# First two weight tiles of the input projection worked in two token parts, with the first loads and the splits put in another order

## What is computed

```python
def rms_norm(x, g):
    xf = x.astype(jnp.float32)
    y = xf * lax.rsqrt(jnp.mean(xf * xf, axis=-1, keepdims=True) + NORM_EPS)
    return (y * g.astype(jnp.float32)).astype(x.dtype)
...
h = rms_norm(xp, norm_mix_pre[l])
z = h @ w_in
```

## Time and profile before

| | |
|---|---|
| median of 3 runs | 893.11 us (892.37 to 893.71) |
| the profiled execution's own time | 894.82 us |
| its span in the trace | 893.0 us |
| PE busy | 865.8 us, 97% |
| DVE busy | 474.3 us, 53% |
| ACT busy | 303.6 us, 34% |
| granted TensorE clock, mean | 0.988 of full |

### The profile page before, as it was taken

How to read it: one execution, slowest core, us unless ns; L and a number is a source line. 1 busy time by engine, 2 the same in 40 slices (tenths; PEclk the granted TensorE clock), 3 DMA queues, 4 the chain that set the end, 5 groups by cost and what they waited for, 6 DMA issues and landing times.

```text
span 893.0 us, 16412 instructions
## 1 busy us (share of the span) xinstructions
PE 865.8 (97%) x6866; PEld 850.1 (95%) x6866; DVE 474.3 (53%) x729; ACT 303.6 (34%) x448; POOL 69.0 (8%) x53
## 2 busy tenths in 40 slices
PE   6999999999999999999996899999999999999997
PEld 6999999999989999999995899999999999999997
DVE  6325779776735546656426654774433443334434
ACT  5211645354531112335323342123311332123432
POOL 1000101100020000000224400000000000000122
PEclk9999999999999999999996999999999999999999
DMA  9322212221313131123231022232222222322212
GB/s 311 105 95 94 86 59 72 88 90 59 96 48 101 54 101 49 54 95 95 95 94 49 18 79 95 95 94 95 82 64 89 94 94 94 94 91 66 80 48 101
DMA packets 77405, 77.28 MB, mean 87 GB/s; under 512 B 2912, under 2 KB 75120, under 8 KB 77360
## 3 DMA queue, kind: packets, MB, share of 16 engines
q1 hardware_dynamic: 68416, 70.53, 24.5%
q10 hardware_dynamic: 8304, 3.95, 1.6%
q0 software_dynamic: 640, 2.17, 0.7%
HBM read 71.64 MB, written 4.99 MB: 86 GB/s over the span
## 4 chain that ended last, share of the span: by engine, by line
PE 92%; DVE 5%; issue 1%; DMA 1%; ACT 1%; SPq 0%; DVEq 0%; ACTq 0%
PE acc L715 76%; PE wk L715 3%; PE wk L739 3%; PE wk L844 3%; DVE act_lo L1372 1%; DMA x_nat<-in_x_prompt 1%; PE wk L805 1%; PE wk L806 1%; PE wk L914 1%; DVE scaled L1353 1%; PE wk L922 1%; DVE w_lo L1065 1%; PE wk L912 0%; PE acc L1043 0%; PE acc L1045 0%
## 5 line engine op out<-in xcount | busy, mean ns | idle before, releaser
L452 ACT ACTIVATE w_hi<-w_raw 128x1024 fp32r<-128x1024 f32 x123 | 130.4, 1060 | 473.8 <-PE acc L715 455.5
L715 PE MATMUL acc<-act_hi,w_hi 128*128 128x272 f32 x1200 | 254.6, 294 | 10.8 <-DVE act_lo L1372 8.6
L715 PE MATMUL acc<-act_hi,w_lo 128*128 128x272 f32 x1200 | 249.8, 290 | 0.0
L715 PE MATMUL acc<-act_lo,w_hi 128*128 128x272 f32 x1200 | 249.1, 289 | 0.0
L715 PEld LDWEIGHTS acc<-act_hi,w_hi 128*128 128x128 f32 x1200 | 190.2, 190 | 16.0 <-DVE act_lo L1372 10.0
L715 PEld LDWEIGHTS acc<-act_lo,w_hi 128*128 128x128 f32 x1200 | 190.3, 190 | 0.0
L715 PEld LDWEIGHTS acc<-act_hi,w_lo 128*128 128x128 f32 x1200 | 188.9, 190 | 0.0
L1065 DVE TENSOR_TENSOR w_lo<-w_raw,w_hi 128x1024 fp32r<-128x1024 f32 x123 | 151.7, 1233 | 35.5 <-ACT w_hi L452 35.0
L715 PE MATMUL acc<-mid_hi,w_hi 128*128 128x272 f32 x480 | 99.0, 287 | 0.0
L715 PE MATMUL acc<-mid_hi,w_lo 128*128 128x272 f32 x480 | 98.7, 288 | 0.0
L715 PE MATMUL acc<-mid_lo,w_hi 128*128 128x272 f32 x480 | 98.6, 287 | 0.0
(11 more groups left out here) (219 smaller groups left out, 985.4 us busy)
## 6 DMA issues: line engine op xcount, KB each, us to landing
w_raw<-in_w_in SPq DMA_DIRECT2D x44, 512.0 KB, 4.4
w_raw<-in_w_ff_up SPq DMA_DIRECT2D x32, 512.0 KB, 4.7
w_raw<-in_w_ff_down SPq DMA_DIRECT2D x32, 512.0 KB, 4.0
w_raw<-in_w_o SPq DMA_DIRECT2D x8, 512.0 KB, 4.5
x_nat<-in_x_prompt SPq DMA_DIRECT2D x4, 512.0 KB, 5.7
w_raw<-in_w_attn_out SPq DMA_DIRECT2D x4, 512.0 KB, 3.6
w_raw<-in_w_ret_out SPq DMA_DIRECT2D x4, 512.0 KB, 4.5
out_y_prompt<-x_nat SPq DMA_DIRECT2D x3, 512.0 KB, 3.1
```

The source lines that it names most:

```text
L452: act.activation(w_hi[:, v % 2], w_raw[:, v // 2, :, P * (v % 2):P * (v % 2) + P], ACT.Copy).then_inc(hi_ready, 1)
L715: ins = pe.matmul(dst[:, n, 0:HALF], w[:, k, :], h[:, HALF * n:HALF * n + HALF], start=begin, stop=end)
```

## The change

The first two weight tiles are worked in two token parts (`PARTS`: tokens 0 to 255, that is x tiles 0 and 1, and tokens 256 to 543, x tiles 2 to 4). PE makes, for weight tile 0 and part 0, first the eight high x high products, then transposes x tile 3, then the products with the low weights, then those with the low x; it transposes x tile 4, does the same for weight tile 1 and part 0, and then part 1 of both tiles. `spread(0)` stands two slabs before the end of the last of these. The loads stand in the order x 0, x 1, first weight tile, x 2, 3, 4, second weight tile, next two weight tiles, key cache. ACT squares x tiles 2 and 3, DVE squares 0, 1 and 4; the squares of tiles 3 and 4, the root and the reciprocal stand behind the splits. `act_hi` and `act_lo` are made in 8 slabs of 256 and 8 of 288 tokens. DVE empties the two tiles in two pieces each.

```diff
@@ sync (SP)
+            load_x(0)
+            load_x(1)
             sp.dma_start(w_raw[:, 0, :, 0:P], w_in_v[:, :, 0:P]).then_inc(w_first, 16)
+            for t in range(2, 5):
+                load_x(t)
             sp.dma_start(w_raw[:, 0, :, P:STAGE], w_in_v[:, :, P:STAGE]).then_inc(w_in_sem[0], 16)
+            load(1, w_in_v[:, 0:4], w_in_v[:, 4:8], STAGE)
             sp.dma_start(k_cache[:], a["cache_attn_k"].rearrange("(t p) c -> p t c", p=P)).then_inc(cache_k_in, 16)
-            load(1, w_in_v[:, 0:4], w_in_v[:, 4:8], STAGE)
@@ scalar (ACT)
+            def x_high(part, copied_act, copied_dve):
+                s, n = PARTS[part]
+                act.wait_ge(x_copied_act, copied_act)
+                act.wait_ge(x_copied_dve, copied_dve)
+                for k in range(KT):
+                    act.activation(act_hi[:, k, s:s + n], xT[:, k, s:s + n], ACT.Copy, scale=gains[:, 0, k:k + 1]).then_inc(x_hi, 1)
+            copy_x(0)
+            act.wait_ge(w_first, 16)
+            split_hi(0, 0)
             act.wait_ge(var_clear, 1)
-            square_sum(1)
-            copy_x(0)
+            square_sum(2)
+            act.wait_ge(gains_in, 16)
+            x_high(0, 1, 1)
+            split_hi(1, 1, 32)
+            copy_x(2)
+            copy_x(4)
+            x_high(1, 3, 2)
             act.wait_ge(x_sum_act, 1)
             square_sum(3)
-            copy_x(2)
-            copy_x(4)
             root(0)
...
@@ tensor (PE)
+            def part_product(j, part, k, w, h, start=False, stop=False):
+                s, n = PARTS[part]
+                return pe.matmul(acc[j][:, part, 0:n], w[:, j, k, :], h[k][:, s:s + n], start=start, stop=stop)
+            def first_part(j):
+                pe.wait_ge(hi_ready, j + 1)
+                for k in range(KT):
+                    pe.wait_ge(x_hi, k + 1)
+                    part_product(j, 0, k, w_hi, H_HI, start=k == 0)
+                if j == 0:
+                    transpose_x(3)
+                pe.wait_ge(lo_ready, j + 1)
+                for k in range(KT):
+                    part_product(j, 0, k, w_lo, H_HI)
+                for k in range(KT):
+                    pe.wait_ge(x_lo, k + 1)
+                    part_product(j, 0, k, w_hi, H_LO, stop=k == KT - 1)
+            def second_part(j):
+                for k in range(KT):
+                    if j and k == KT - 2:
+                        pe.wait_ge(x_copied_act, 3)
+                        spread(0)
+                    pe.wait_ge(x_hi, KT + k + 1)
+                    part_product(j, 1, k, w_hi, H_HI, start=k == 0)
+                    part_product(j, 1, k, w_lo, H_HI)
+                    pe.wait_ge(x_lo, KT + k + 1)
+                    ins = part_product(j, 1, k, w_hi, H_LO, stop=k == KT - 1)
+                ins.then_inc(mm_done, 1)
+            first_part(0)
+            transpose_x(4)
+            first_part(1)
+            second_part(0)
+            second_part(1)
@@ vector (DVE)
             square_sum(0)
-            square_sum(2)
+            square_sum(1)
             copy_x(1)
+            split_lo(0, 0)
+            x_low(0)
+            copy_x(3)
+            split_lo(1, 1)
+            x_low(1)
             square_sum(4)
...
```

More of the change, by code:

```diff
@@ L302, in x_psum @@
                 return wk[:, 1024 * (t - 2):1024 * (t - 1)].rearrange("p (k c) -> p k c", k=KT)
-            return acc[0][:, 0, 0:KT * n].rearrange("p (k c) -> p k c", k=KT)
+            return wk[:, 0:KT * n].rearrange("p (k c) -> p k c", k=KT)
         PART_TILES = (range(0, 2), range(2, 5))
@@ L330, in _, with load_x @@
         def _(sp):
-            for t, (s, n) in enumerate(TILES):
+            def load_x(t):
+                s, n = TILES[t]
                 src = a["x_prompt"][0, s:s + n, :] if t < 4 else a["x_sample"][0]
@@ L482, in root @@
                 act.activation(tok_rstd[:, cols], tok_var[:, cols], ACT.Sqrt).then_inc(std_ready, 1)
-            act.wait_ge(var_clear, 1)
-            square_sum(1)
-            copy_x(0)
+            def x_high(part, copied_act, copied_dve):
[7 more added lines that the diff above has]
+            split_hi(0, 0)
+            act.wait_ge(var_clear, 1)
+            square_sum(2)
[5 more added lines that the diff above has]
+            x_high(1, 3, 2)
             act.wait_ge(x_sum_act, 1)
             square_sum(3)
-            copy_x(2)
-            copy_x(4)
             root(0)
[L493 to L501, removed]
             split_ahead(0, 0)
@@ L742, in _, with transpose_x @@
             pe.wait_ge(ident_in, 16)
-            for t, (s, n) in enumerate(TILES):
+            def transpose_x(t):
+                s, n = TILES[t]
                 pe.wait_ge(x_in[t], 16)
                 if t == 4:
-                    pe.wait_ge(x_copied_act, 1)
+                    pe.wait_ge(x_copied_act, 2)
                 ps = x_psum(t)
@@ L751, in _ @@
                 ins.then_inc(x_tr, 1)
+            for t in range(3):
+                transpose_x(t)
             def feature_sum(norm, added, squares, tiles=range(5)):
@@ L1090, in copy_x, with x_low @@
                 dve.tensor_copy(xT[:, :, s:s + n], x_psum(t)).then_inc(x_copied_dve, 1)
+            def x_low(part):
+                s, n = PARTS[part]
+                for k in range(KT):
+                    dve.wait_ge(x_hi, KT * part + k + 1)
+                    dve.scalar_tensor_tensor(act_lo[:, k, s:s + n], xT[:, k, s:s + n], gains[:, 0, k:k + 1],
+                                             act_hi[:, k, s:s + n].bitcast(fp), ALU.mult, ALU.subtract).then_inc(x_lo, 1)
             square_sum(0)
-            square_sum(2)
+            square_sum(1)
             copy_x(1)
+            split_lo(0, 0)
[3 more added lines that the diff above has]
+            x_low(1)
             square_sum(4)
@@ L1098, in _ @@
             dve.tensor_scalar(tok_var[:, 0:5], tok_var[:, 0:5], 1.0 / D, EPS, ALU.mult, ALU.add).then_inc(var_ready, 1)
-            copy_x(3)
             dve.wait_ge(std_ready, 1)
             dve.reciprocal(tok_rstd[:, 0:5], tok_rstd[:, 0:5]).then_inc(tok_rstd_ready, 1)
[L1102 to L1107, removed]
             dve.wait_ge(spread_mm, 1)
@@ L1132, in attention_inputs @@
                     split_ahead(g, j)
-            with dve.Fori(0, G_RET - 1) as g:
-                attention_inputs(g)
+            for j in range(2):
+                dve.wait_ge(mm_done, j + 1)
+                for part, (s, n) in enumerate(PARTS):
+                    ins = dve.tensor_tensor(z[:, j, s:s + n], acc[j][:, part, 0:n], rstd[:, s:s + n], ALU.mult)
+                ins.then_inc(acc_free, 1)
+                split_ahead(0, j)
+            for j in range(2, 4):
+                to_z(0, j, j)
+                split_ahead(0, j)
+            attention_inputs(1)
             dve.wait_ge(hankel_in, 16)
```

## The result

The changed kernel takes 897.09 us, median of 20 runs (895.40 to 898.93). The kernel before takes 893.65 us in 20 runs beside it (892.04 to 896.16). The ratio is 1.0035, interval 1.0027 to 1.0043: about 3.1 to 3.4 us slower, by ratio or by medians. The prediction said 893.9 us and at most 895.5.

What follows compares the result with a forecast made beforehand. PE, busy 97% of the span, bounds the kernel. Tile 2 at 30.4 us plus 1.2 us for the clock gives 31.6 against 30.79, 0.8 us later: 893.9 us, range 892.6 to 895.5.

Steps and rivals of the forecast that it cites:

- the clock term: PE's start: the lower clock behind the slab-paced products costs 1.2 us, bounds 0 and 2.6 us.
- rival A: PE's thin early work keeps the clock low for two stretches: tile 2 +2.2 us, total 895.3 us; chance 0.13.
- The bound of 2.6 us: Upper bound of the clock's cost at PE's start, if the lower level lasts 5 us more behind the paced products.
- the clock's cost before: Kernel before, first products: 3.3 us at the lower clock, some 7 pairs, costing 1.4 to 1.5 us.
- The measure itself: PE's start of weight tile 2, 30.79 us before: a shift of this moment is the shift of the total.
- The structure: Start to weight tile 2 without clock cost: DVE decides, tile 2 at 30.4 us, 0.4 us earlier than before.
- the slabs: ACT's eight `act_hi` slabs of 256 tokens take 0.39 us each, ends 0.31 and 0.42; they end at 14.2 us.
- The loads: First weight tile lands at 8.2 us, x tile 2 at 10.0 us, bounds 9.4 and 10.6.
- PE's bound work at full clock: PE from the last high x high product to the spread's end: 13.0 us, ending at 27.4 us.
- DVE's tail: Behind the spread DVE does `rstd`, two pieces of `z` and the low part of weight tile 2: 2.9 us.
- The key cache: Moved behind two weight tiles, lands at worst at 22.6 us; PE needs it at 28 us: no cost.
- Rival B: Transposes don't wake PE's clock: 2.5 us at the start, +2.1 us, total 895.2 us; chance 0.05.

Runs made afterwards that it cites:

- filler: Added identity transposes in PE's gaps that change nothing computed; changed kernel with it 894.64 us, ratio 1.0011; kernel before with it 893.63 us, 0.9998, then 893.43, 0.9982.
- again-runs: Both kernels run and profiled a second time without edits: before 893.32 us, ratio 0.9996; changed 896.68 us, ratio 1.0036.
- a_again: Changed kernel a second time, no edit: 896.68 us, ratio 1.0036.
- a_x3in: Changed kernel with only the transposes of x 3 moved between the fifth and sixth product of weight tile 0: 894.65 us, ratio 1.0003.
- a_sq_warm: Changed kernel with the squares of x 2 behind the first eight `act_hi` slabs and idle transposes in PE's gaps: 894.68 us, ratio 1.0011.
- a_spread4: Changed kernel with the spread at slab 3 of the last token part instead of 6: 896.86 us, ratio 1.0034.
- a_sqlate: Changed kernel with ACT's squares of x 2 moved behind the first eight slabs of `act_hi`: 894.87 us, ratio 1.0009.
- a_fit2: The kernel of `a_fit` a second time: 894.01 us, ratio 0.9997.
- b_warm: Kernel before with idle identity transposes on PE around the spread: 893.63 us, ratio 0.9998.
- the second run with the new loads: Kernel before with only the new order of the loads, run again: 897.56 us, ratio 1.0042.
- a_oldloads: Changed kernel with the loads in the order of the kernel before: 900.19 us, ratio 1.0065.
- b_again: Kernel before a second time, no edit: 893.32 us, ratio 0.9996.
- a_fit: Changed kernel, x 3's transposes between fifth and sixth product, ACT's squares behind all slabs, copy of x 2 ahead of second weight split: 892.67 us, ratio 0.9984.

## Why the prediction was wrong

**The step that failed is the clock term,** "I take 1.2 us, a little less than the 1.5 it costs now", and with it the chance of 0.13 for rival A. Rival A had the mechanism: the thin work leaves the clock low, two stretches follow one another, and part of the dense work runs at half speed. The stretch is 6.8 us, of which 4.1 us cost 2.05 us in the profile; by medians, filler gives back 2.0 to 2.4 us. I argued that a part of the stretch would fall on the paced products, where it is free. That was right (2.7 us did), but I took the stretch to be one of 3.3 us. The paced products didn't use it up: it went on behind the slabs, in both profiles of the changed kernel. The bound of 2.6 us that I had set held. In the profile this is 0.85 us of the 1.2 us by which tile 2 came later than forecast (27.66 us behind the first transpose, forecast 26.46).

**The other half of the same step is the clock's cost before.** I took 1.5 us from one profile. Two sets of runs with filler give 0.2 and 1.6 us. So the difference between after and before wasn't 1.2 - 1.5 = -0.3 us but about 2.2 - 0.9 = +1.3 us.

**The measure itself was too narrow.** "All behind it is the same work on a PE that doesn't wait, so a shift of this moment is the shift of the total": the work is the same, but its length isn't fixed, and tile 2 moved by 1.6 to 2.0 us while the total moved by 3.1 to 3.4. What the profiles show behind tile 2 stands under "What stays open".

**The structure** was to cost 1.1 us without the clock (0.4 us earlier than before, which had 1.5 of the clock in it). With both kernels kept busy, the medians differ by 1.0 to 1.2 us, the ratios by 1.3 to 2.9 thousandths (mean 1.9 us), and T2 by 1.3 to 1.7 us. So it was right or somewhat low. Two parts of it are visible after: the slabs took 0.41 us each (0.39 forecast, inside the bounds of 0.31 and 0.42), and the first product started 0.55 us behind the start of its slab, where the forecast (11.1 and 11.2) had left out the slab's own length. From the first slab to the first ready work it is 3.7 us, not 3.3.

**The rest, point by point.** The loads: x 2 was forecast at 10.0; ACT takes it at 10.85 in the profile with the 0.86 us offset, right. PE's bound work at full clock, 13.0 us: it took 15.2 us (15.62 to 30.82), 2.05 of them for the clock, and where the clock was full each piece had the length forecast (products of 288 columns 0.133 us apart, x 4's transposes 0.6, the spread 1.3). DVE's tail: 2.9 us forecast, 2.8 measured; the handoff of tile 2 waits 0.16 us for `w_lo`, just under the forecast of 0.2 to 0.6. The key cache: no wait. Rival B, transposes that don't wake the clock, is refuted by more than the earlier trace rows now: in the changed kernel with filler PE does nothing but transposes ahead of its first product, the twelve of the identity among them take 1.47 us, and behind the filler eight transposes of x 3 take 1.03 us. The Trainium skill's rule, "TensorE: Matmul & The Clock Gate", Part 4, that PE's transpose mode doesn't count as being busy for the clock, is not what these runs show (it stands there beside a measurement in bf16; the transposes here are float32).

Range and chances: half of rival A's price was in the range and its chance was 0.13, so 895.5 was the upper end. Rival A in full would not have saved the forecast: its shift of tile 2, 2.2 us, is near the measured 1.6 to 2.0, but its 895.3 is still too low, since it took before's clock at 1.5 us too and counted nothing behind tile 2. The sum of the measured terms would have been: structure +1.1 to 1.9, clock +1.3: 2.4 to 3.2 us, 895.5 to 896.3 from the median that was known. The medians ended at 896.7 and 897.1, of which 0.5 is a kernel before that measured 893.65 in the later runs. These terms are differences of the measured times and add up by their making; they say where the loss lies, and are no second proof of it.

**What stays open.** T2 moved by 1.6 us (again-runs) to 2.0 us (first profiles), the medians by 3.1 to 3.4. The remaining 1 us or so lies behind tile 2, where both kernels do the same work. There all 18 profiles agree but for three places and some 0.5 us at the very end. At 250 to 256 us a stretch at half clock costs 1.5 us (in `a_again`, `a_x3in` and `a_sq_warm`). From some 470 to 500 us, where all have a long one of 10 to 20 us at half clock and PE waits a good part of the time (busy for 9.8 of 17 us before), the time to its end differs by up to 1.7 us. At 500 to 508 us a stretch costs 1.25 us (after, `a_spread4`, `a_sqlate`, `a_fit2`, and in the kernel before `b_warm` and the second run with the new loads). `a_oldloads` has a fourth behind these, of 1.6 us. From tile 2 to the chain's row of 384 products at about 425 us it is 395.0 to 395.1 us in both kernels, wherever the stretch at 250 us is missing. So what differs behind tile 2 in the profiles goes with the clock again. With one profile per run I can't say whether a changed start makes these stretches likelier or whether they fall by chance.

## What to carry to other kernels

To start a bound engine earlier on work that another engine doles out can cost more than it gains, if the engine leaves this thin stretch at the lower clock and then runs its ready work at half speed. Put work that has to be done anyway into the gaps, ahead of the ready work, as moving eight transposes did here for 2 us and more; and price the clock as a separate term, with what a thin stretch adds to the length of the low one. Before a clock stretch of one profile goes into a sum, ask a second profile, a median or the granted clock of the other executions whether it is there each time.

## What the runs showed of the hardware

- At the first products the lower level lasted 3.4 us in some profiles (15.1 to 18.5 in `b_again`, 12.3 to 15.7 in `a_fit`), 6.8 us in others (12.9 to 19.7 after, 11.3 to 18 in `a_spread4`), and some 10 us in `a_oldloads` (11.9 to 22). Each time PE had been idle or its work thin just before.
- Transposes of an identity matrix in PE's gaps left the products behind them at full clock (pairs of 272 columns 0.25 us apart in `b_warm`, against 0.45 before), and no loss from them shows in the medians (893.63 and 893.43 us in the kernel before).
- The column of the granted clock says 1.00 up to the first change that the trace holds, even where the spacing shows the lower level: the first 16 transposes of x take 3.3 to 3.7 us in every profile here, about 0.22 us apart where eight later ones take 1.1, and in `a_again` the transposes of x 2 and x 3 are slow under a clock of 1.00. Until then the spacing of equal instructions is the better clock.
- In the kernel before an execution's time goes with its mean granted clock: 892.1 us at 0.992, 894.6 at 0.988.
- The same kernel differed by 1.2 to 1.4 us by ratio from one set of runs to the next (0.9984 and 0.9997; 0.9998 and 0.9982, 11 or 12 executions each). Differences below this need more than two sets.
